# Sample attention ahead of the prompt's blocks, and the last prompt block between layer 1's expert slots

## The chip, the cores and the metric

The kernel runs on one core of one Trainium2 chip. The time is that of one execution on the device, in microseconds (us). Three runs of the kernel before took 3454.8, 3460.62 and 3466.63 us; the median is 3460.62 us. The engines are TensorE (PE, with its weight loads as PEld), VectorE (DVE), ScalarE (ACT), GpSimd (POOL) and SyncE (SP), which only issues DMAs. Each runs its own instructions in the order of the program and waits on semaphores for the others.

## The reference

One inference step of a two-layer decoder for 512 prompt tokens and 8 sample tokens (rows of 1024 floats). What matters here:

```python
x = s5_layer(x)                     # layer 0: state space mixer
x = x + ga2 * peer(h, layer 0)      # experts
ckv, kr = shared_kv(x)              # latent keys and values, 256 + 32 wide
# layer 1: latent attention, 16 heads
s = (q_lat . ckv + q_pe . kr) * SM_SCALE   # causal, in blocks of 128 queries, for the prompt
o = softmax(s) . ckv                       # the samples: over 2048 paged cache rows and their own
x = x + ga1 * (o . w_ukv) @ w_o
x = x + ga2 * peer(h, layer 1)
def peer(h):                        # 8 heads, top 16 of 128 x 128 keys each: 128 experts a token
    s = (h @ w_q) . sub_keys; idx, g = top_k(top_k(s, 16) pairs, 16), softmax
    u, v = u_emb[idx], v_emb[idx]   # rows of 1024 floats each
    return sum_k g * gelu(h . u) * v
```

## The kernel before

**The expert stage.** The 512 prompt tokens are four tiles of 128 tokens, the samples are a fifth, smaller tile; `t` counts them over both layers, 0 to 4 in layer 0 and 5 to 9 in layer 1. A prompt tile has 128 slots, one for each chosen expert: in a slot, POOL's indirect DMA (L1133) fetches a row of `peer_uv` for each of the 128 tokens (1 MB: 128 partitions, 2048 floats), DVE makes the dot product (L2143), ACT the gelu, its gate and a diagonal (L1411, L1421, L1424), and PE adds the value rows with 16 matmuls (L2747). The rows lie in a ring of six buffers; slot m+6 is fetched when PE has freed the buffer of slot m. What is computed for the next tile (norm, turn, 16 `query` groups L2681, `score` L2707, and `top` on DVE L2059 ff, in six parts for a head) is spread by `peer_plan` (L457) over the slots of the tile that runs: a list of steps that each engine walks, doing those that are its own. `PLAN[0]` is layer 0's, `PLAN[1]` layer 1's.

**The stretch between the layers.** With the last tiles of layer 0 most of the projections of attention are already computed. Between the two lists stand hand written sequences, one for each engine: `attention_sync` (L1036, SP), `attention_pool` (L1156), `attention_act` (L1612), `attention_dve` (L2337) and `attention_pe` (L2912). Their order is: the samples' latent queries (L2918); 8 key products (L2928); 4 value products (L2942); then a pipelined loop over 64 head steps, 16 heads in each of prompt blocks 0 to 3 (block i sees i+1 tiles of keys): scores L2958 and mask L2962 on PE, maximum L2363 on DVE, exponential L1638 on ACT, reciprocal L2368 on DVE, scaling L1154 on POOL (`scaled_probabilities`), transposes L2972 on PE, copies L2375 on DVE, and the product with the values L3067 on PE, a pair of heads at a time (`pair_outputs`). After each block follows the output projection `project` (L3107, L3116) and `attention_out` on DVE. Then come the samples, one after the other over 2048 cache rows each (`cache_turn` L3085, `cache_scores` L3098 and L3102, L3001, L3014); their rows are fetched by POOL (L1174, L1177) into three buffers. `merge` joins the partial sums (L3019 to L3050), `sample_project` (L3130) projects them. The norm, the first query group, the first score and the first head's `top` of tile 5 are computed during the samples and the merge (the list `EARLY`). Layer 1's gathers start when the first head's experts are known.

SP fetches prompt queries, weights and rows in the order of its own list; a wait there holds back all that follows.

## Time and profile before

| | us |
|---|---|
| median of three runs (3454.8 to 3466.63) | 3460.62 |
| the profiled execution | 3468.7 |
| its span, first to last instruction | 3466.6 |
| PE busy in it | 2561.7 |
| DVE busy in it | 2331.3 |
| ACT busy in it | 1252.6 |
| POOL busy in it | 1239.8 |
| mean granted TensorE clock, share of full | 0.804 |

The span holds both expert stages, which the indirect DMAs fill, and what lies before, between and after them. Stretches are given in us from the start of the span. A line of a timeline has start, duration, engine, line, operation and its operands, the count, and in brackets the idle time before it with what ended it.

### The profile page before, as it was taken

The numbers are of one execution on the slowest core, as the hardware profiler recorded it, in microseconds if no ns is written. First come the engines' busy times: TensorE is split into PE (matmuls) and PEld (weight loads), VectorE is DVE, ScalarE is ACT, GpSimd is POOL, SyncE is SP. The second block draws the span as 40 slices with busy tenths as digits, with TensorE's granted clock in tenths as the row PEclk, the third lists the DMA queues.
The fourth block names the chain that finished last, engine by engine and source line by source line (L and its number), as shares of the span: only waits on it lengthen the run. The fifth ranks groups of instructions, "written<-read, shape, count | busy, mean of one in ns | idle before, by whom it ended". The sixth has DMA issues, their size and how long they took to land.

```text
span 3466.6 us, 62653 instructions
## 1 busy us (share of the span) xinstructions
PE 2561.7 (74%) x25173; PEld 936.6 (27%) x25173; DVE 2331.3 (67%) x5471; ACT 1252.6 (36%) x3861; POOL 1239.8 (36%) x1133
## 2 busy tenths in 40 slices
PE   4878997767668766668889986686686677666666
PEld 3756322323003100112235563240040023001000
DVE  8753885897775776465644455978767767775655
ACT  3442333333333333344432232433433343334333
POOL 0010343444444444334413512344444444443432
PEclk8979998878778766779998998797686678667677
DMA  9966999999999999999950157999999999999997
GB/s 321 354 228 269 394 419 415 409 400 407 426 425 409 413 426 423 408 414 410 389 176 29 74 213 314 403 408 421 426 397 426 426 423 411 427 424 403 422 427 318
DMA packets 182783, 1276.32 MB, mean 368 GB/s; under 512 B 22200, under 2 KB 27808, under 8 KB 35544
## 3 DMA queue, kind: packets, MB, share of 16 engines
q0 software_dynamic: 151696, 1109.99, 77.6%
q1 hardware_dynamic: 30224, 161.80, 12.5%
q8 instruction: 195, 3.19, 0.3%
q14 instruction: 92, 0.75, 0.1%
q10 hardware_dynamic: 576, 0.59, 0.0%
HBM read 1260.89 MB, written 11.40 MB: 367 GB/s over the span
## 4 chain that ended last, share of the span: by engine, by line
DMA 37%; PE 36%; DVE 18%; ACT 6%; issue 3%; POOL 1%; SPq 0%; DVEq 0%; ACTq 0%; PEldq 0%; POOLq 0%
DMA arena<-peer_uv,arena 35%; PE psum L2747 12%; DVE arena L2143 8%; PE psum L2681 7%; PE psum L2640 3%; PE psum L3116 2%; DMA arena<-b_mod 2%; PE psum L2897 1%; PE psum L2828 1%; ACT arena L1424 1%; ACT arena L1421 1%; DVE arena L2154 1%; PE psum L2508 1%; DVE arena L2059 1%; DVE arena L1714 1%
## 5 line engine op out<-in xcount | busy, mean ns | idle before, releaser
L2747 PE MATMUL psum<-arena 32*32 32x512 f32 x16384 | 1491.5, 801 | 743.7 <-ACT arena L1424 733.2
L1133 POOL DMA_INDIRECT arena<-peer_uv,arena x1040 | 1134.9, 1091 | 1782.6 <-PE psum L2747 1527.7
L2143 DVE SCALAR_TENSOR_TENSOR arena<-arena 128x1024 f32<-128x1024 f32 x1040 | 1272.4, 1225 | 730.4 <-DMA arena<-peer_uv,arena 716.1
L1411 ACT ACTIVATE arena<-arena 128x1 f32<-128x1 f32 x1040 | 210.3, 202 | 1528.8 <-DVE arena L2143 1524.1
L2747 PEld LDWEIGHTS psum<-arena 32*32 32x32 f32 x16384 | 214.9, 118 | 1877.6 <-ACT arena L1424 1771.9
L1424 ACT ACTIVATE arena<-arena 128x32 f32<-128x32 f32 x1024 | 329.1, 321 | 33.4
L1421 ACT ACTIVATE arena<-arena 128x1 f32<-128x1 f32 x1040 | 306.0, 294 | 33.8
L2681 PEld LDWEIGHTS psum<-arena 128*128 128x128 f32 x2048 | 244.9, 197 | 78.7 <-issue 75.8
L2681 PE MATMUL psum<-arena 128*128 128x128 f32 x2048 | 263.9, 285 | 2.7 <-ACT arena L1363 2.2
L2640 PE MATMUL psum<-arena 128*128 128x512 f32 x256 | 126.7, 628 | 3.2 <-ACT arena L1321 2.4
L2508 PE MATMUL psum<-arena 128*9 128x128 f32 x2048 | 82.3, 325 | 59.4 <-DMA arena<-b_mod 59.3
L1154 POOL TENSOR_SCALAR arena<-arena 128x128 f32<-128x128 f32 (+3 forms) x64 | 68.8, 1082 | 93.9 <-DVE arena L2368 93.2
L1714 DVE TENSOR_TENSOR arena<-arena 128x512 f32<-128x512 f32 (+9 forms) x177 | 89.3, 505 | 8.7 <-ACT arena L1201 2.8
L2143 DVE DVE_READ_ACCUMULATOR arena<-arena 128x1 f32 x1040 | 84.8, 82 | 0.0
L2508 PEld LDWEIGHTS psum<-arena 128*9 128x9 f32 x2048 | 62.3, 106 | 75.2 <-issue 43.0
L1638 ACT ACTIVATE arena<-psum,arena 128x128 f32<-128x128 f32 (+3 forms) x64 | 33.7, 527 | 105.9 <-DVE arena L2363 105.7
L2059 DVE MAX8 arena<-arena 128x8 f32<-128x128 f32 (+1 forms) x204 | 61.8, 331 | 13.1 <-ACT arena L1456 10.8
L2640 PEld LDWEIGHTS psum<-arena 128*128 128x128 f32 x256 | 45.8, 194 | 83.8 <-issue 79.4
L2059 DVE FIND_INDEX8 arena<-arena 128x8 uint32<-128x128 f32 (+1 forms) x204 | 65.5, 329 | 0.0
L2061 DVE FIND_INDEX8 arena<-arena 128x8 uint32<-128x128 f32 (+1 forms) x204 | 65.5, 329 | 0.0
L2060 DVE MATCH_REPLACE8 arena<-arena 128x128 f32<-128x128 f32 (+1 forms) x204 | 64.2, 320 | 0.0
L1223 ACT ACTIVATE arena<-psum 9x128 f32<-9x128 f32 x128 | 34.4, 269 | 76.7 <-PE psum L2513 74.2
(350 smaller groups left out, 2298.2 us busy)
## 6 DMA issues: line engine op xcount, KB each, us to landing
arena<-w_mod SPq DMA_DIRECT2D x64, 1024.0 KB
arena<-peer_wq SPq DMA_DIRECT2D x12, 2048.0 KB, 11.6
arena<-peer_uv,arena POOLq DMA_INDIRECT x1040
arena<-w_glu SPq DMA_DIRECT2D x5, 2048.0 KB
arena<-mod_rows SPq DMA_DIRECT2D x4, 1024.0 KB
arena<-w_o SPq DMA_DIRECT2D x1, 4096.0 KB
arena<-mod_rows SPq DMA_DIRECT2D x7, 512.0 KB
arena<-x_after_layer SPq DMA_DIRECT2D x7, 512.0 KB
```

Of the source, the lines that this page charges most:

```text
L1133: pool.indirect_dma_start(ring[r], None, a[f"peer_uv{t // 5}"], bass.IndirectOffsetOnAxis(ap=ix, axis=0)).then_inc(landed[r], 16)
L1411: act.activation(col, col, ACT.Gelu_apprx_tanh).then_inc(s_gl, 1)
L1421: act.activation(wcol, col, ACT.Copy, scale=gate_).then_inc(s_gl, 1)
L1424: act.activation(diag[:, n_ % RING, :], eye32, ACT.Copy, scale=wcol).then_inc(s_dg, 1)
L1714: link(dve.tensor_tensor(out, x, y, op))
L2059: steps = (lambda x, v, i: dve.max(v[:, 0:8], x), lambda x, v, i: dve.max_index(i[:, 0:8], v[:, 0:8], x), lambda x, v, i: dve.match_replac ...
L2143: dve.scalar_tensor_tensor(out=u, in0=u, scalar=1.0, in1=h, op0=ALU.mult, op1=ALU.mult, accum_out=at(DOTS + (t % 2) * 2 * P + m, 1)).then_ ...
L2508: ins = pe.matmul(mod_bank(b, q, one), silu[:, k, :], w[k // 4][:, k % 4, MQ4 * q:MQ4 * (q + 1)], start=(k == 0), stop=False, skip_group_c ...
L2640: ins = pe.matmul(psum[:, unit_bank(u), :], ztk[:, k, P * j:P * (j + 1)], w[:, k, :], start=(k == 0), stop=(k == KD - 1))
L2681: ins = pe.matmul(psum[:, 4 + m % 2, P * q:P * q + R], (wq[:, m, k] if t else wide(WQ0[m])[:, k])[:, P * q:P * (q + 1)], htr[:, k, 0:R], s ...
L2747: ins = pe.matmul(acc_of(t, i, c), diag[rows, r, :], ring[r][rows, D + 512 * c:D + 512 * (c + 1)], start=(m == 0), stop=last, skip_group_c ...
L3116: ins = pe.matmul(psum[:, 5 + n_, :], ot[:, k, :], wo[:, k, 512 * n_:512 * (n_ + 1)], start=(k == 0), stop=(k == KD - 1))
```

## The change

The stretch between the layers is put in another order, and a part of it is moved into layer 1's expert stage.

The samples come first, right after their latent queries; the key products are spread over the merge, the value products lie around the samples' projection. Then comes a new list, `exposed_blocks`, of 48 head steps for prompt blocks 0 to 2, as `PLAN[1]`. From its step 21 on it also holds the whole front of tile 5: norm, turn, 16 query groups (with two buffers of their own for the weights, in the ring), four scores, and `top` of heads 0 and 1. Layer 1's first six gathers are issued after the 48th scaling on POOL. Block 3 (16 heads, projection in four pieces) becomes steps in the first 46 slots of tile 5 (`blocks_in_stream`); the other six heads of `top` of tile 5 follow at 2.4 slots a part, those of tile 6 are split between tile 5 and tile 6. The head steps 16 to 47 use two score banks for three, and one transpose bank for two. SP reads block 3's queries back from memory as it does those of the other blocks; layer 1's query weights are fetched twice: in pieces for tile 5 between the layers (8 MB), and again for tiles 6 to 9 during the slots of tile 5 (8 MB). Of these 16 MB the kernel before fetches 8.

```diff
-            first = [[] for _ in range(64)]
-            prep(t0, first, 0)
-            ahead = 21 if layer else 26
-            for steps in first[:ahead]:
-                plan += steps
-            plan += [("top", t0, 0, part) for part in range(6)]
...
+                if t == 5:
+                    blocks_in_stream(extra)
+                    for m in range(36):
+                        extra[1 + int(2.4 * m)].append(("top", t, 2 + m // 6, m % 6))
+                    for m, h0 in ((29, 2), (60, 4), (90, 6)):
+                        extra[m].append(("shift", t, h0, h0 + 2))
+                        extra[m + 1].append(("exps", t, h0, h0 + 2))
+                        extra[m + 2].append(("gates", t, h0, h0 + 2))
...
-                    at_ = 73 if t == 0 else 40 if b == 0 else 10
+                    at_ = 73 if t == 0 else 76 if b == 0 else 10
                     prep(t + 1, extra, at_)
                     at_ += 22 if b < 3 else 30
-                    gap = 1.25 if t == 0 else 1.3 if b == 0 else 1.5 if b == 3 else 1.75
-                    heads = 4 if t == 0 else heads_of(t + 1)
+                    gap = 1.25 if t == 0 else 1.1 if b == 0 else 1.5 if b == 3 else 1.75
+                    heads = 4 if b == 0 else heads_of(t + 1)
                     for m in range(6 * heads):
...
-        EARLY = ([(what, 5) for what in ("squares", "means", "roots", "norm", "shifted", "turned")]
-                 + [("turn", 5, 0), ("turn", 5, 1), ("queried", 5, 0), ("score", 5, 0), ("scored", 5, 0)]
-                 + [("query", 5, 0, q) for q in range(4)] + [("top", 5, 0, part) for part in range(6)])
-        PLAN = [peer_plan(0), [step for step in peer_plan(1) if step not in EARLY]]
...
+        INS = 3
+        EXPOSED = INS * NH
...
+        def blocks_in_stream(extra):
+
+            for i in range(INS, NTILE):
+                base = 1 if i == INS else 41
+                for p in range(NH // 2):
+                    n, s = NH * i + 2 * p, base + 4 * p
+                    extra[s].append(("pscore", n))
+                    extra[s + 1].append(("pscore", n + 1))
+                    extra[s + 3] += [("pmax", n), ("pmax", n + 1)]
+                    extra[s + 4] += [("pscale", n), ("pscale", n + 1)]
+                    extra[s + 5].append(("pturn", n))
+                    extra[s + 7] += [("pturned", n), ("pturn", n + 1)]
+                    extra[s + 9] += [("pturned", n + 1), ("pvalue", n // 2)]
+                    if p % 4 == 3:
+                        extra[s + 11].append(("pheads", n // 8))
+                for piece in range(4):
+                    extra[base + 40 + piece].append(("project", i, piece))
+                extra[base + 45].append(("pout", i))
...
+        def exposed_blocks():
+
+            t, plan, queries = 5, [], [("query", 5, m, q) for m in range(4) for q in range(4)]
+            side = [[] for _ in range(EXPOSED + 8)]
+            side[21] += [("squares", t), ("means", t)]
+            side[22] += [("roots", t), ("norm", t)]
+            side[23] += [("shifted", t), ("turn", t, 0), ("turn", t, 1), ("turned", t)]
+            for k, step in enumerate(queries):
+                side[24 + k // 2].append(step)
+                if step[3] == 3:
+                    m = step[2]
+                    side[24 + k // 2].append(("queried", t, m))
+                    side[25 + k // 2] += [("score", t, m)]
+                    side[26 + k // 2] += [("scored", t, m)]
+            for k in range(12):
+                side[29 + k // 2].append(("top", t, k // 6, k % 6))
+            side[35] += [("shift", t, 0, 2), ("exps", t, 0, 2), ("gates", t, 0, 2)]
+            for it in range(EXPOSED + 8):
+                if it < EXPOSED:
+                    plan += [("pscore", it), ("pmax", it)]
+                if it >= 5 and it % 2 and it - 5 < EXPOSED:
+                    p = (it - 5) // 2
+                    plan.append(("pvalue", p))
+                    if p % 4 == 3:
+                        plan.append(("pheads", p // 4))
+                if 1 <= it <= EXPOSED:
+                    plan.append(("pscale", it - 1))
+                if 3 <= it < EXPOSED + 3:
+                    plan += [("pturn", it - 3), ("pturned", it - 3)]
+                if it % NH == 4 and it >= NH:
+                    i = it // NH - 1
+                    plan += [("project", i, piece) for piece in range(4)] + [("pout", i)]
+                plan += side[it]
+            return plan
...
+        def pscore_bank(n):
+
+            if n < NH:
+                return (0, 1, 7)[n % 3]
+            return (n + 1) % 2 if n < EXPOSED else 4 + n % 2
+
+        def pturn_bank(n):
+
+            if n < NH:
+                return 2 + 4 * (n % 2)
+            return 2 if n < EXPOSED else 6
+
+        def pvalue_bank(p):
+            return 3 if 2 * p < EXPOSED else 7
+
+        def project_bank(i):
+            return 6 if i >= INS else 4
+
+        BLOCKS = 1
...
+        PLAN = [peer_plan(0), exposed_blocks(), peer_plan(1)]
...
-                for dst, src, rows in ((WK, "w_k", P), (WV, "w_v", P), (WKT, "w_kt", NOPE)):
+                for dst, src, rows in ((WV, "w_v", P), (WKT, "w_kt", NOPE)):
                     n_ = a[src].shape[1]
                     sp.dma_start(at(dst, n_, 0, rows), a[src]).then_inc(s_lw, 16)
+                queries_spill(3)
...
+                for g in range(4):
+                    sp.dma_start(at(X4, 256, 32 * g, 32 * g + NB), x2s_dram[:, 256 * g:256 * (g + 1)]
+                                 ).then_inc(s_mw, 16)
+                    sp.dma_start(at(GAS4, 256, 32 * g, 32 * g + NB),
+                                 mod_dram[1:NC9, 8 * D + 256 * g:8 * D + 256 * (g + 1)]).then_inc(s_mw, 16)
                 sp.dma_start(at(WO, KD * D), a["w_o"]).then_inc(s_mw, 16)
...
+                sp.dma_start(at(WK, 2 * NH * NOPE), a["w_k"]).then_inc(s_mw, 16)
+                sp.dma_start(at(GAP, D), mod_dram[0:1, 8 * D:9 * D].partition_broadcast(P)).then_inc(s_mw, 16)
+
                 sp.wait_ge(s_cpv, NB)
+                block_queries(0)
+                first_query_weights(0)
+                first_query_weights(1)
+                sp.wait_ge(s_mg, 7)
+                block_queries(1)
+                sp.dma_start(at(SSB, D), a["g_norm"][3:4, :].partition_broadcast(P)).then_inc(s_pmod, 16)
+                sp.wait_ge(s_ktp, NH // 2)
+                sp.dma_start(at(PMOD, 2 * D), mod_dram[0:1, 9 * D:11 * D].partition_broadcast(P)
+                             ).then_inc(s_pmod, 16)
+                sp.wait_ge(s_vp, NTILE)
+                block_in(0)
+                block_in(1)
+                sp.wait_ge(s_mh, 2)
                 peer_keys(1)
-                sp.wait_ge(s_yy, 5)
-                peer_weights(1, 2)
-                peer_weights(1, 3)
-                attention_store(4)
-                for i in range(2):
-                    sp.wait_ge(s_rst[i], row_no(STORES, "residual", 4 - i))
-                    sp.wait_ge(s_kvs[i], 32 * (3 - i))
-
-            def attention_store(j):
-                sp.wait_ge(s_x3, j + 1)
-                if j < 4:
-                    sp.dma_start(x3_dram[P * j:P * (j + 1)], at(MX + (j % 2) * D, D)).then_inc(s_rst[j % 2], 16)
-                    return
+                sp.wait_ge(s_x3, 1)
                 for g in range(4):
                     sp.dma_start(x3s_dram[:, 256 * g:256 * (g + 1)], at(X4, 256, 32 * g, 32 * g + NB)
                                  ).then_inc(s_rst[0], 16)
+                block_out(0)
+                sp.wait_ge(s_S, NH)
+                block_queries(2)
+                sp.wait_ge(s_pq, 21)
+                first_query_weights(2)
+                sp.wait_ge(s_pq, 22)
+                first_query_weights(3)
+                sp.wait_ge(s_ph, 6)
+                block_stored(0)
+                block_in(3)
...
+            def blocks_beside_experts(load):
+
+                block_out(2)
+                block_stored(2)
+                load(6)
+                sp.wait_ge(s_S, 4 * NH)
+                peer_weights(1, 0)
+                peer_weights(1, 1)
+                sp.wait_ge(s_pv, NTILE * NH // 2)
+                final_loads()
+                sp.dma_start(at(HSP, D), a["g_norm"][3:4, :].partition_broadcast(P)).then_inc(s_pmod, 16)
+                sp.wait_ge(s_yy, NTILE + 1)
+                peer_weights(1, 2)
+                peer_weights(1, 3)
+                block_out(3)
+                sp.wait_ge(s_kvs[0], 96)
+                sp.wait_ge(s_kvs[1], 64)
+                sp.wait_ge(s_rst[0], row_no(STORES, "residual", 4))
+                sp.dma_start(at(PMOD + 2 * D, D), mod_dram[0:1, 11 * D:12 * D].partition_broadcast(P)
+                             ).then_inc(s_pmod, 16)
+                sp.dma_start(at(PMOD + 3 * D, 3 * D, 0, NB), mod_dram[1:NC9, 9 * D:12 * D]).then_inc(s_pmod, 16)
+                block_stored(3)
+                load(5)
 
             peer_tiles(0, x1_dram, x1s_dram, x2_dram, x2s_dram)
             attention_sync()
-            peer_loads(1)
             peer_tiles(1, x3_dram, x3s_dram, a["out_y_p"], a["out_y_s"])
...
                 for b in range(NB):
                     if b == 1:
-                        scaled_probabilities()
-                        pool.wait_ge(s_pv, NTILE * NH // 2)
-                    if b == 3:
-                        pool.wait_ge(s_rz, 1)
+                        pool.memset(at(QRZ, NB * P), 0.0).then_inc(s_rz, 1)
+                        pool.wait_ge(s_qsp, 64)
...
+            def second_gather(k):
+
+                t, m = (5 + k // P, k % P) if k < NTILE * P else (9, k - NTILE * P)
+                if t == 9:
+                    if m == 0:
+                        pool.wait_ge(s_sld, 32)
+                    gather(t, m, at(IXS, SGRP).bitcast(I32)[:, m:m + 1])
+                    return
+                if m % TOPK == 0:
+                    pool.wait_ge(s_idx, 8 * t + m // TOPK + 1)
+                if k < RING:
+                    r = slot_no(t, m) % RING
+                    if r >= 4:
+                        pool.wait_ge(s_S, NH * (3 if r == 4 else 2))
+                    else:
+                        pool.wait_ge(s_pq, 23 + r // 2)
+                gather(t, m, at(IDXP + (t % 2) * P, P).bitcast(I32)[:, m:m + 1])
+
+            def second_gathers():
+                total, k = NTILE * P + SGRP, RING
+                for ahead in range(RING):
+                    second_gather(ahead)
+                for what, *which in PLAN[2]:
+                    if what == "pscale":
+                        scaled_probabilities(*which)
+                    elif what == "slot" and k < total:
+                        second_gather(k)
+                        k += 1
 
             peer_gathers(0)
             attention_pool()
-            peer_gathers(1)
+            blocks_pool()
+            second_gathers()
```

## Rows read from the trace of the kernel before

**Rows 1.** The page, 40 slices of the span: what the DMA engines moved.
```profile
GB/s 321 354 228 269 394 419 415 409 400 407 426 425 409 413 426 423 408 414 410 389 176 29 74 213 314 403 408 421 426 397 426 426 423 411 427 424 403 422 427 318
```

**Rows 2.** Busy time by stretch; the last columns are the clock, DMA share, GB/s.
```profile
1900.00:2000.00 100.00, 91.61 (x523) 52.25 (x522) 45.79 (x98) 23.66 (x61) 44.42 (x33) 0.99 0.18 69
2400.00:2500.00 100.00, 66.88 (x648) 9.03 (x640) 80.92 (x178) 43.03 (x133) 43.46 (x40) 0.67 1.01 422
```

**Rows 3.** POOL's timeline around the stretch between the layers.
```profile
1732.32 1.86 POOL L1133 DMA_INDIRECT arena<-peer_uv,arena  x1 [2.31 <-PE psum L2752]
...
1928.92 2.81 POOL L1154 TENSOR_SCALAR arena<-arena 128x384 f32<-128x384 f32 x2 [1.12 <-DVE arena L2368]
...
2102.06 0.94 POOL L1133 DMA_INDIRECT arena<-peer_uv,arena  x1 [46.95 <-DVE arena L2109]
...
2121.87 1.14 POOL L1133 DMA_INDIRECT arena<-peer_uv,arena  x1 [12.67 <-PE psum L2747]
```

**Rows 4.** PE's timeline of the same stretch.
```profile
1804.02 1.92 PE L2918 MATMUL psum<-arena 64*8 64x256 f32 x32 [1.79 <-ACT arena L1604]
1805.87 14.00 PE L2928 MATMUL psum<-arena 128*128 128x512 f32 x32
...
1834.32 0.38 PE L2958 MATMUL psum<-arena 96*128 96x128 f32 x2
...
1858.92 13.90 PE L3116 MATMUL psum<-arena 128*128 128x512 f32 x32
...
2003.37 1.92 PE L3098 MATMUL psum<-arena 128*32 128x512 f32 x16
...
2079.65 0.27 PE L3019 MATMUL psum<-arena 128*8 128x128 f32 x1
...
2081.14 3.84 PE L2681 MATMUL psum<-arena 128*128 128x128 f32 x32 [1.11 <-ACT arena L1363]
...
2091.07 1.16 PE L2707 MATMUL psum<-arena 128*128 128x128 f32 x8
...
2103.30 6.23 PE L3130 MATMUL psum<-arena 128*8 128x256 f32 x64 [0.31 <-ACT arena L1670]
```

**Rows 5.** DVE's timeline: attention_out's last pass, the first head's top, a dot.
```profile
1995.15 1.23 DVE L2488 TENSOR_TENSOR arena<-arena 128x1024 f32<-128x1024 f32 x1
...
2093.24 0.48 DVE L2059 MAX8 arena<-arena 128x8 f32<-128x128 f32 x2
...
2101.62 0.17 DVE L2109 SCALAR_TENSOR_TENSOR arena<-arena 128x16 int32<-128x16 f32 x1
...
2112.89 1.22 DVE L2143 SCALAR_TENSOR_TENSOR arena<-arena 128x1024 f32<-128x1024 f32 x1
```

**Rows 6.** The cache gathers of L1174, issue to landing, all eight.
```profile
DMA to landing us min/median/max: 7.9/8.2/11.6
```

**Rows 7.** DMA issues from 1700 to 2200 us: layer 1's query weights.
```profile
arena<-peer_wq SPq DMA_DIRECT2D x4, 2048.0 KB, 7.1
```

**Rows 8.** Busy time by stretch, columns as rows 2: block 3, the start of layer 1.
```profile
1949.40:1977.90 28.50, 25.84 (x218) 16.62 (x216) 19.47 (x39) 9.04 (x23) 18.62 (x12) 1.00 0.05 20
...
2100.00:2125.00 25.00, 19.39 (x202) 11.62 (x202) 14.18 (x48) 5.77 (x17) 7.97 (x9) 0.85 0.86 348
```

**Rows 9.** ACT's timeline beside slots: an exponential between two gelus.
```profile
2243.70 1.28 ACT L1403 ACT_TABLE_LOAD   x1
2245.00 0.26 ACT L1403 ACTIVATE arena<-arena 128x64 f32<-128x64 f32 x1
2245.27 1.28 ACT L1411 ACT_TABLE_LOAD   x1
```

**Rows 10.** PE beside a tile's query groups: one slot, half its queries, the next slot.
```profile
2529.93 1.09 PE L2747 MATMUL psum<-arena 32*32 32x512 f32 x16
...
2530.95 2.05 PE L2681 MATMUL psum<-arena 128*128 128x128 f32 x16
...
2532.93 1.09 PE L2747 MATMUL psum<-arena 32*32 32x512 f32 x16
```

683 lines of the change are left out of this document (359 added, 324 removed).

## The prediction, made before the changed kernel ran

> **What bounds the kernel now.** I read the page's slices first: the DMA engines move some 400 to 427 GB/s through most of the span, with one hole in the middle [rows 1]. The stretches say how deep: in steady slots the DMA share is 1.01 at 422 GB/s, with PE busy 67% and DVE 81%, while between the layers it is 0.18 and PE is busy 92% [rows 2]. So the expert stages run at the gathers' pace: 40 gathers in 100 us, 2.5 us each [rows 2]. POOL's timeline gives the hole's edges: layer 0's last gather is issued at 1732.3, layer 1's first at 2102.1 [rows 3], and from there to the end of the span are 1364.5 us. Only two things can change the time: when that first gather leaves (I call it G), and what the rest costs after it, in bytes or in slots that fall behind.
>
> The sum is made against the profiled span, 3466.6 us; the execution took 3468.7, and the median of the runs, 3460.6, lies 6.0 below the span. Layer 0 keeps its list, and up to 1804 only loads and a store of SP change, which nothing on that path waits for; I cost it at nothing, at worst 2 us.
>
> **The new G, stage by stage.** The starting point is the latent queries at 1804.0 [rows 4].
>
> *Samples.* Before, from the first sample's scores at 2003.4 to the merge at 2079.7 are 76.3 us [rows 4]; about 1 of them is tile 5's turn, which goes. New is that the cache rows must land first. The gather is issued at about 1803. Landing takes 7.9 to 11.6 us [rows 6], the long one beside w_o; here w_o is issued some 4 us behind it, so I take 9: PE waits until 1812 (bounds 1811 to 1815). Nothing hides this; what was hidden there (keys and values) is now later. For the first sample's turns, copies and latent transposes ahead of its scores I take what a whole further sample takes, 76.3 / 8 or about 10 us: 1822. Then 75.3: the merge begins at 1897 to 1898. The second and third cache rows, w_o and w_k are some 11 MB in the queue at 1808, 27 us at 422 GB/s, against a need at about 1835: 0 to 5 us, I take 1. 1898.
>
> *Merge with keys.* Keys cost 14.0 us on PE [rows 4]. The merge itself: from 2079.7 to the samples' projection at 2103.3 are 23.7 us, less two times two query groups (7.7), the score (1.2) and the wait for `top` (2093.2 to 2101.8) leaves about 6 [rows 4, 5]. The keys take the query groups' place as filler. 19.5 together, to 1917.5.
>
> *Values and the samples' projection.* Values take as much as keys, 14. The projection's 6.23 us [rows 4] ran behind G and now stand ahead of it. With transposes 20.5, to 1938; DVE's last copy and the masks add 2: head steps run from 1940.
>
> *48 head steps.* Before, they ran from 1834.3 to the 48th scaling, the first of the two in the row at 1928.9, which ends at about 1930 [rows 3, 4]: 96 us, with two projections of 13.90 in them. The third projection and block 3 fall behind G: that is the gain. Fewer banks put a copy between two transposes, which lies beside the next scores; PE was idle a tenth of the loop [rows 8], so I allow nothing to 0.15 us for each of 32 steps, bounds 0 and 5, and take 1.
>
> *Tile 5's front in them.* At steps 21 to 23: norm, shift and the scale's preparation are four DVE passes of about 1.2 us (as the 1.23 of [rows 5]), behind a square root on ACT with its table, 1.3 us each way [rows 9]; 5.5 us. From 24 to 31 PE has 16 query groups, 3.84 us for four [rows 4], 15.4 in all, and 4 scores of 1.16. DVE does two heads of `top` in steps 29 to 34; one head takes 8.5 us, 2093.2 to 2101.8 [rows 5], so 17. Head steps tie the engines together within one or two steps, so the fuller engine sets each: PE in steps 24 to 28 (5 steps of 1.9 for queries and 0.6 for scores, 12.5, less 1 for its idle share), DVE in 29 to 34 (17 less 1.3, which hide the other queries): 27. The third and fourth weight pieces are fetched when a buffer is free; 7.1 us to land [rows 7] against two steps of together 7 us (1.4 a step of the loop's own and 2.5 of the front's): 1. Gates, by the step's own size, 1.5. Together 35, bounds 22 (PE's work alone) and 44.
>
> G = 1940 + 96 + 1 + 35 = 2072, 30 earlier than before.
>
> **After G.** Before, this took 1364.5 us. Four things are added.
>
> *More bytes.* Before, query weights 2 and 3 (4 MB), mods, gains and rows, 8.6 MB, are loaded behind G. Now it is all four weights again (8 MB) and the rest, 13.1. The difference, 4.5 MB (4.7 million bytes), costs 11 us at 422 GB/s; no cover, as DMA is the bound. Bounds 8 and 13.
>
> *A hole behind the first six.* Six gathers are 15 us of DMA. Before, PE freed the first buffer 19.8 us after G (2121.9) [rows 3], and weights filled the gap: the first 25 us, 2 of them ahead of G, average 348 GB/s [rows 8]. Now, behind the 48th scaling come the last transposes and values (two head steps and a copy, 3.4 us), the third projection (13.9 [rows 4]) and attention_out (2 x 1.23 [rows 5]): DVE's first dot stands at G+20 (before G+10.8 [rows 5]), behind it ACT, PE and the issue take some 5 us, and data flows again at about G+26.5 against a drained queue at G+17. A row of 0.5 MB comes in between: 9 us lost, bounds 5 and 12.
>
> *Block 3 in 45 slots.* Its loop took 25.8 us of PE in 28.5 [rows 8] for three quarters of the heads, some 37 us for all with projection apart. For every 4 slots (10 us) PE has 4 x 1.09 [rows 10] and 4.6 for two heads, 9.0; DVE has 4 dots of 1.22 [rows 5], 1.67 parts of `top` (8.5 / 6 each) and 2.7 for two heads (19.5 of DVE less 2.5 of attention_out for 12 or 13 heads [rows 8]), 10.0; POOL 4 gathers of 0.94 [rows 3] and two scalings of 1.5 (18.6 for 12 [rows 8]), 6.8. DVE is just full, but behind the 31st slot 8 MB of weights slow the gathers and it catches up. The projection puts 3.5 us on PE in each of 4 slots, while the ring holds 15 us. I take 4 us, bounds 0 and 24.
>
> ACT now alternates between gelu and exp: the row shows 1.28 us for a table and the next activation 1.30 after its start, both ways [rows 9]. Eight pairs of heads make 16 loads, 21 us, beside 112 us of slots in which ACT is under half busy [rows 2]; they cost nothing, or 2 us. The Trainium skill, in "ScalarE: Activation LUTs", section "Table sets: the hidden batching unit", has a rule against this part ("Batch activation calls by set, not by function"), and its section "What ACT_TABLE_LOAD costs" puts 2.66 us to a switch with its drain. The row shows 1.30, so the trace does not agree with the larger figure; by the Trainium skill's figure the 16 loads would be an estimated 43 us of ACT, still beside other work.
>
> *Less work later.* Twelve parts of `top` leave the slots. They were under the gathers: nothing.
>
> After G: 1364.5 + 11 + 9 + 4 = 1388.5. End: 2072 + 1388.5 = 3460.5, 6 under the old span; against the median 3454.6, rounded 3454.
>
> **The rivals.**
>
> *The stretch between is shorter.* PE idles about a tenth of the head steps, and part of the queries and of `top` may fall into those gaps (25 us for the front of tile 5 in place of 35), the samples run without tile 5's steps and wait less (4 less), the hole is 5. For it: PE's busy share there was 25.8 of 28.5 [rows 8], so there is room. Against it: in steps 29 to 34 DVE alone has its 17 us, and the list is in order. 3454 - 10 - 4 - 4 = 3436.
>
> *The mixed slots become the bound (slower).* Place: PE and DVE in slots 1 to 45 of tile 5. Where a tile's queries stand beside slots, PE's cycle is 3.0 us from one slot to the next (2529.9 to 2532.9) although its parts are 1.09 and 2.05 [rows 10]; the same order of work, scores, transposes, values, waits among them, might hold block 3's slots at 3.1. It decides once four slots take over 10 us on PE or on DVE; DVE has nothing to spare, and a wait for the exponential (1.3 + 2 x 0.9) stands in its list. Price: 0.6 x 45 = 27 in place of 4: 3454 + 23 = 3477. Against it: PE's average is under the pace, and six buffers even it out.
>
> *The change does not bring the samples forward as it says*: the first cache rows queue behind w_o and the spill, and the next ones behind these. Price 10 us, if w_o's 4 MB and the two others go first; 3464. For it: the 11.6 us landing [rows 6]. The Trainium skill, in "DMA: Bandwidth & Descriptors", section "SWDGE vs HWDGE vs iDMA", says that an engine goes round robin between its queues, so a gather would not stand behind w_o, but share with it; no row here shows the order within an engine.
>
> **How the numbers follow.** Forecast (3444 to 3466) 0.47, the shorter stretch 0.28, mixed slots 0.19, late cache rows 0.06. A difference of under about 0.3%, 10 us, can't be told from none in this kernel: that is 3450 to 3471. Of the forecast 0.10 lies under 3450. Faster: 0.28 + 0.10 = 0.38. Slower: 0.17 of the mixed slots, 0.02 of the late rows: 0.19. The same: 0.43. The range takes in the short stretch with the bounds of the front's cost (3430) and the mixed slots to their price (3477): 3430 to 3477. The likeliest case's own range is 3444 to 3466.
>
> **What the profile of the changed kernel would show.** The first cache turn on PE at about 1812, the first merge transpose near 1898, the first L2958 scores near 1940, and POOL's first peer gather at 2072 (2056 for the shorter stretch, over 2080 for late cache rows). A DMA share well under 1 for about 9 us from G+17. In the first 110 us of slots DMA at 400 GB/s or more; if PE or DVE is the bound, the share falls to 0.8 to 0.9 and DVE waits for PE or ACT, not for the gathers. From there to the end, the same pace as before. The prediction is wrong if G lies outside 2060 to 2085, or if what follows G is outside 1378 to 1400 us.

## The result, and the profile after

The changed kernel took 3488.4 us (median of four runs, 3484.1 to 3493.9) against 3457.7 for the kernel before (median of four): the medians lie 30.7 us apart, and the ratio with its 95% interval is put at 1.0075 (1.005 to 1.010), which is 26 us. It is slower by 26 to 31 us, where 3454 had been forecast, and the time lies above the range of 3430 to 3477. Its profiled execution took 3490.1 us with a span of 3487.9 and a mean granted clock of 0.803.

The page's slices answer [rows 1]. The hole between the layers has moved forward, and at its end stands a slice of 321 that lies wholly behind the first gather (2092 to 2180 us); four slices on, one of 382 is new.

```profile
GB/s 319 346 233 273 397 419 416 414 402 410 426 424 408 421 426 425 409 419 398 351 186 211 80 101 321 410 418 404 382 405 424 426 417 410 426 424 380 423 427 320
```

PE's timeline answers [rows 4]. To read in it: the latent queries at 1798.0, the wait for the first cache rows (11.36 us on a DMA), the merge at 1899.7, the keys, values from 1919.3, the first block's scores at 1937 to 1939, and then in the head steps the query groups of tile 5 (L2836) and their score (L2865).

```profile
1798.01 1.92 PE L3088 MATMUL psum<-arena 64*8 64x256 f32 x32 [1.78 <-ACT arena L1754]
1811.29 3.65 PE L3279 MATMUL psum<-arena 128*128 128x128 f32 x16 [11.36 <-DMA arena<-cache_kr,arena]
1827.70 4.53 PE L3279 MATMUL psum<-arena 128*128 128x128 f32 x20 [4.84 <-DMA arena<-cache_kr,arena]
1899.71 0.27 PE L3134 MATMUL psum<-arena 128*8 128x128 f32 x1
1900.38 3.67 PE L3196 MATMUL psum<-arena 128*128 128x512 f32 x8 [0.29 <-ACT arena L1791]
1919.26 7.13 PE L3206 MATMUL psum<-arena 128*128 128x512 f32 x16
1938.83 0.23 PE L3231 MATMUL psum<-arena 128*128 128x128 bf16 x1 [1.36 <-DVE arena L2521]
...
2003.52 3.74 PE L2836 MATMUL psum<-arena 128*128 128x128 f32 x32
2007.94 1.16 PE L2865 MATMUL psum<-arena 128*128 128x128 f32 x8
2008.94 3.74 PE L2836 MATMUL psum<-arena 128*128 128x128 f32 x32
```

POOL's timeline answers [rows 3]: the first gather of layer 1 at 2080.3 (before 2102.1), the first refill of the ring 27.3 us behind it (before 19.8), and a pair of block 3's scalings (L1269) between the gathers, on the same engine.

```profile
2080.28 1.01 POOL L1249 DMA_INDIRECT arena<-peer_uv,arena  x1 [0.16 <-issue]
...
2107.57 1.30 POOL L1249 DMA_INDIRECT arena<-peer_uv,arena  x1 [20.07 <-PE psum L2909]
2110.40 0.94 POOL L1249 DMA_INDIRECT arena<-peer_uv,arena  x1 [1.53 <-PE psum L2909]
...
2120.45 3.11 POOL L1269 TENSOR_SCALAR arena<-arena 128x512 f32<-128x512 f32 x2
2123.72 0.99 POOL L1249 DMA_INDIRECT arena<-peer_uv,arena  x1 [0.17 <-issue]
```

Two lengths carry the comparison, since layer 0's end moves from one profiled execution to the next: the latent queries came at 1798.0 and 1810.1 in two profiles of the changed kernel. The **front** is the time from the latent queries to the first gather of layer 1 (G): 298.0 us before [rows 3, 4], 282.3 after. The **tail** is the time from G to the end of the span: 1364.5 before, 1407.6 after. The front gained 15.7, the tail lost 43.1, and the two make +27.4, about what the whole times show. (From 1804.0 the forecast had 268 for the front and 1388.5 for the tail.)

Where the tail lost it is read from the gathers, one a slot, numbered from G in POOL's timeline. Us after G:

| gather | before | after |
|---|---|---|
| 16 | 52.9 | 56.8 |
| 32 | 102.0 | 103.5 |
| 48 | 144.8 | 155.8 |
| 64 | 185.5 | 212.3 |
| 96 | 266.2 | 292.8 |
| 128 (tile 6's first) | 345.0 | 375.0 |
| 144 | 387.0 | 426.0 |
| end of the span | 1364.5 | 1407.6 |

30.0 us go by gather 128, another 9.1 in tile 6's first 16 slots, and 4.1 in all the rest (0.6 in a second profile of the changed kernel, so this part is no loss). The stretches between gathers of the table (columns as in [rows 2]), first of after, gathers 0 to 16, 16 to 48, its two halves 16 to 32 and 32 to 48, 128 to 144, and the bottom of the dip; then of before, gathers 128 to 144:

```profile
2080.28:2137.06 56.78, 43.52 (x301) 16.03 (x297) 30.75 (x72) 22.43 (x55) 25.30 (x20) 0.88 0.78 297
2137.06:2236.08 99.02, 73.90 (x711) 27.27 (x709) 72.61 (x186) 51.42 (x133) 56.44 (x44) 0.88 0.97 382
2137.06:2183.78 46.72, 36.58 (x381) 14.44 (x379) 39.23 (x95) 29.04 (x73) 32.17 (x25) 0.93 0.94 355
2183.78:2236.08 52.30, 37.32 (x332) 12.83 (x331) 33.38 (x92) 22.38 (x62) 24.26 (x20) 0.84 1.00 406
2455.24:2506.30 51.06, 29.09 (x264) 3.98 (x272) 45.63 (x117) 21.30 (x60) 19.35 (x16) 0.57 0.96 378
2100.00:2110.00 10.00, 5.18 (x38) 1.11 (x36) 9.30 (x25) 2.46 (x9) 1.30 (x1) 0.83 0.37 116
```

```profile
2447.03:2489.03 42.00, 27.84 (x272) 4.04 (x272) 31.86 (x51) 22.52 (x62) 17.90 (x16) 0.65 1.01 425
```

The first two rows are the stretch in which block 3 sits. 32 slots took 99.0 us, **3.09 us a slot**, where [rows 2] have 2.5. The two halves differ: 2.92 us a slot at a share of 0.94, then 3.27 at a share of 1.00 and 406 GB/s, when two planes of query weights (4 MB, issued at 2194) come beside the gathers. So the engines hold back the transfers in the first 32 slots, and in the next 16 the transfers are full. In tile 6's first slots VectorE is busy 45.6 of 51.1 us, before 31.9 of 42.0: the 24 parts of `top` that now stand there at 1.2 slots each.

The DMA answer over 128 gathers gives the bytes, after first and then before:

```profile
DMA packets 19878, 145.55 MB, mean 388 GB/s; under 512 B 2201, under 2 KB 2201, under 8 KB 3097
```

```profile
DMA packets 19355, 141.28 MB, mean 410 GB/s; under 512 B 2170, under 2 KB 2202, under 8 KB 2714
```

4.27 MB more cost 10.4 us at 410 GB/s (an estimate); the other 19.6 of the 30.0 are the lower rate.

What VectorE waits for longest between 2137 and 2183 us, in total, times and longest; after, after between 2183 and 2236 us, and then before:

```profile
DVE arena L2555 <- PE psum L3247: 6.0, 2, 3.8
```

```profile
DVE arena L2278 <- DMA arena<-peer_uv,arena: 16.1, 7, 5.1
```

```profile
DVE arena L2143 <- DMA arena<-peer_uv,arena: 11.5, 8, 2.6
```

Before, VectorE waited for gathers, so the transfers were the bound. After, it waits for none in the first of its stretches; it waits for TensorE's transposes of block 3 (L3247). In the second it waits for gathers again, 16.1 us. One turn of the loop is seen whole in the timeline of all engines (start, duration, engine, line):

```profile
2130.66 4.46 POOL L1269 TENSOR_SCALAR arena<-arena 128x512 f32<-128x512 f32 x2
...
2133.16 1.28 ACT L1809 ACT_TABLE_LOAD   x1
2133.63 0.66 PE L3247 MATMUL psum<-arena 128*128 128x128 f32 x4 [1.54 <-POOL arena L1269]
...
2134.32 0.69 DVE L2555 COPY arena<-psum 128x512 f32<-128x512 f32 x1 [2.09 <-PE psum L3247]
2134.93 1.28 DVE L2539 TENSOR_REDUCE arena<-psum 128x1 f32<-128x512 f32 x2
...
2135.64 0.69 ACT L1809 ACTIVATE arena<-psum,arena 128x512 f32<-128x512 f32 x1 [1.20 <-DVE arena L2539]
...
2137.11 1.28 ACT L1557 ACT_TABLE_LOAD   x1
...
2138.40 0.20 ACT L1557 ACTIVATE arena<-arena 128x1 f32<-128x1 f32 x1
...
2139.34 1.09 PE L2909 MATMUL psum<-arena 32*32 32x512 f32 x16 [1.68 <-ACT arena L1570]
...
2140.77 0.94 POOL L1249 DMA_INDIRECT arena<-peer_uv,arena  x1 [1.37 <-PE psum L2909]
```

Each bracket names the engine above it: TensorE's transpose waits for POOL's scaling, VectorE's copy for the transpose, the exponential for VectorE's maxima, the slot's matmul for ScalarE behind the table load that follows the exponential, and the gather for that matmul. No engine is full (TensorE is busy 75% and VectorE 73% of these 32 slots), and each works through its list in order, so a wait for one block step also holds back the expert slot that stands behind it.

### The profile page after: what moved, and what is told of

Read it like the earlier page. It is cut to its first block and busy times, and to the rows that moved or that the text cites. A ratio compares the mean times of both kernels' runs of the same rounds, so it can differ in the third digit from the quotient of the medians.

```text
span 3487.9 us, 62696 instructions
## 1 busy us (share of the span) xinstructions
PE 2562.2 (73%) x25173; PEld 938.6 (27%) x25173; DVE 2330.3 (67%) x5474; ACT 1274.6 (37%) x3880; POOL 1251.7 (36%) x1133
## 5 line engine op out<-in xcount | busy, mean ns | idle before, releaser
L1570 ACT ACTIVATE arena<-arena 128x32 f32<-128x32 f32 x1024 | 329.1, 321 | 33.4
L2836 PE MATMUL psum<-arena 128*128 128x128 f32 x2048 | 259.5, 282 | 1.1 <-ACT arena L1509 1.1
L2836 PEld LDWEIGHTS psum<-arena 128*128 128x128 f32 x2048 | 241.9, 195 | 68.4 <-issue 66.7
L1269 POOL TENSOR_SCALAR arena<-arena 128x128 f32<-128x128 f32 (+3 forms) x64 | 73.2, 1148 | 134.5 <-DVE arena L2546 133.3
L1809 ACT ACTIVATE arena<-psum,arena 128x128 f32<-128x128 f32 (+3 forms) x64 | 33.5, 526 | 102.5 <-DVE arena L2539 102.3
## 6 DMA issues: line engine op xcount, KB each, us to landing
arena<-peer_uv,arena POOLq DMA_INDIRECT x1040, 10.2
```

The lines of the kernel that those rows point to most:

```text
L1269: pool.tensor_scalar(pp, pp, at(SUMS + n_ % 16, 1), None, ALU.mult).then_inc(s_sc, 1)
L1570: act.activation(diag[:, n_ % RING, :], eye32, ACT.Copy, scale=wcol).then_inc(s_dg, 1)
L2836: ins = pe.matmul(psum[:, 4 + m % 2, P * q:P * q + R], (wq1[m][:, k] if t == 5 else wq[:, m, k] if t else wide(WQ0[m])[:, k])[:, P * q:P * ...
```

## The experiments

All start from the changed kernel. Lengths are from one profiled execution each; the changed kernel was run twice (*control*), and its two profiles give 282.3 and 281.3 for the front, 375.0 and 374.3 for gather 128, 1407.6 and 1403.4 for the tail. The tail holds to about 4 us, and the ratio to the kernel before has intervals of about 0.25% either way. Gather 128 is the sharpest measure, but less sharp than these two profiles make it. Seven kernels that change nothing ahead of G (*spread6*, *turnlate*, *notable*, *dve2*, *pe2*, *copy_act*, *relief*) show a front of 278.3 to 279.0. The same head steps ran there at a mean granted clock of 0.91 and in the changed kernel at 0.89, which took 3.3 us more from the masks to G. In these seven the ring's first refill also comes 25.7 us behind G and not 27.3. So differences of under 2 us at gather 128 are read as none.

| kernel | front | gather 16 | 32 | 48 | 128 | 128 to 144 | tail | ratio to before |
|---|---|---|---|---|---|---|---|---|
| before | 298.0 | 52.9 | 102.0 | 144.8 | 345.0 | 42.0 | 1364.5 | 1 |
| after | 282.3 | 56.8 | 103.5 | 155.8 | 375.0 | 51.1 | 1407.6 | 1.0075 [1.0050, 1.0100] |
| control | 281.3 | 56.8 | 104.4 | 155.9 | 374.3 | 51.1 | 1403.4 | 1.0082 [1.0052, 1.0112] |
| ins4 | 328.4 | 61.6 | 100.8 | 140.1 | 342.4 | 51.4 | 1370.4 | 1.0122 [1.0092, 1.0151] |
| spread6 | 278.3 | 54.1 | 98.0 | 145.6 | 378.8 | 52.4 | 1406.0 | 1.0083 [1.0057, 1.0109] |
| proj2 | 281.8 | 40.4 | 89.7 | 144.6 | 371.6 | 51.0 | 1401.0 | 1.0080 [1.0053, 1.0108] |
| balanced | 282.8 | 55.8 | 104.7 | 158.2 | 376.7 | 45.4 | 1397.5 | 1.0060 [1.0037, 1.0083] |
| late3 | 282.7 | 50.0 | 89.2 | 138.5 | 377.9 | 51.5 | 1404.3 | 1.0103 [1.0083, 1.0123] |
| turnlate | 278.6 | 53.1 | 100.7 | 152.3 | 372.1 | 51.1 | 1406.1 | 1.0098 [1.0077, 1.0118] |
| scale_act | 282.0 | 55.2 | 100.6 | 154.2 | 373.0 | 52.0 | 1400.6 | 1.0085 [1.0058, 1.0111] |
| notable | 278.4 | 54.2 | 98.1 | 151.1 | 370.5 | 51.5 | 1397.8 | 1.0067 [1.0046, 1.0087] |
| dve2 | 278.3 | 57.2 | 107.7 | 159.5 | 378.9 | 51.1 | 1408.1 | 1.0102 [1.0073, 1.0132] |
| pe2 | 279.0 | 54.6 | 104.1 | 157.0 | 377.4 | 51.4 | 1402.8 | 1.0080 [1.0046, 1.0114] |
| copy_act | 278.4 | 55.9 | 107.0 | 158.8 | 379.4 | 52.2 | 1409.4 | 1.0081 [1.0057, 1.0105] |
| tiny | 282.8 | 49.4 | 92.4 | 144.2 | 364.2 | 51.4 | 1392.8 | 1.0042 [1.0022, 1.0062] |
| relief | 278.3 | 50.2 | 91.5 | 143.9 | 364.7 | 51.0 | 1391.3 | 1.0035 [1.0019, 1.0051] |
| wqhole | 282.8 | 63.2 | 111.0 | 160.6 | 379.7 | 51.0 | 1407.5 | 1.0101 [1.0074, 1.0128] |
| front2q | 307.1 | 54.9 | 102.8 | 154.7 | 376.4 | 51.1 | 1406.5 | 1.0156 [1.0117, 1.0195] |
| combo3 | 273.6 | 42.2 | 93.7 | 141.8 | 368.3 | 45.1 | 1389.2 | 1.0000 [0.9978, 1.0022] |
| combo4 | 273.7 | 42.1 | 89.0 | 137.0 | 361.4 | 45.1 | 1381.7 | 0.9997 [0.9981, 1.0012] |

> The changed kernel again, for the spread of the two stretches between profiled executions: from the latent query to the first gather of layer 1 282.3, from there to the end 1407.6. Every theory expects both again within 4 us, and the time within 3482 to 3496.

The front and gather 128 held, the tail at the edge of the 4 us; the median, 3495.3, stood against 3466.5 for the kernel before beside it.

**Is it block 3 in the slots?** *ins4* puts block 3 back between the samples and the first gather and keeps all else.

```
-        INS = 3
+        INS = 4
```

> The changed kernel with INS = 4: block 3 goes back between the layers as head steps 48 to 63 of the exposed list, nothing of it lies in tile 5's slots. G is the issue of layer 1's first gather (2080.3 in the changed kernel), R what follows it to the end of the span (1407.6; before 1364.5). Theory A (of R's 43 us more, about 13 are block 3 in the slots and 10 a hole of the DMA behind the first six gathers): G rises by 16 heads (37) and the third projection (14) to about 2131, R falls to about 1385, as weights can fill the hole; time 3518. Theory B (the repeated 8 MB and DMA traffic alone make R long, the mixed slots cost nothing): R stays at 1400 or more, time 3532 or more.

Its windows over gathers 0 to 16 and 16 to 32:

```profile
2132.32:2193.95 61.63, 37.41 (x255) 11.05 (x258) 24.63 (x59) 11.70 (x38) 15.85 (x16) 0.72 1.00 414
2193.95:2233.17 39.22, 23.71 (x256) 3.06 (x240) 28.90 (x71) 13.07 (x48) 16.99 (x16) 0.75 1.01 426
```

The transfers never let up: no dip and no slow slots, although the same query weights are loaded again. The ring's first refill is nearly as late as in the changed kernel (26.5 us behind G), but here block 3's scores are done early, so SP issues the first two planes of weights 4 us ahead of G and the other two 20 us behind it:

```profile
2128.12 0.81 SPq L981 DMA_DIRECT2D arena<-peer_wq  x2
```

These bytes fill the gap. The tail is 1370.4, only 6 over before's, although tile 6's first slots take 9 more. So block 3 in the slots, with the later weights that come of it, costs the tail 33 to 37 us (gather 128: 375.0 against 342.4), while the front is 46.1 longer without it (328.4 against 282.3). Theory A had the direction and not the size (1385 and 3518 said, 1370.4 and 3504.7 measured). The move of block 3 brings 9 to 14 us by itself, of the 46 that it takes from the front. And the rest of the change, which *ins4* has too, costs 36 us by the profiles (30.4 in the front, where all of tile 5's front now stands ahead of G, and 5.9 in the tail): that is why the whole is slower although this move pays. The row also gives the price of a slot at full rate: 39.22 / 16 = 2.45 us.

**Is it the dip at the start?** Three kernels. *late3* starts block 3's steps at slot 29, *spread6* puts six slots instead of four between pairs of heads, *proj2* puts block 2's projection into slots 1 to 4 and starts block 3 at slot 8.

```
 late3    -                base = 1 if i == INS else 41
          +                base = 29 if i == INS else 41
 spread6  -                    n, s = NH * i + 2 * p, base + 4 * p
          +                    n, s = NH * i + 2 * p, base + 6 * p
          -                    extra[base + 40 + piece].append(("project", i, piece))
          +                    extra[base + 54 + piece].append(("project", i, piece))
 proj2    +                for piece in range(4):
          +                    extra[1 + piece].append(("project", i - 1, piece))
          +                extra[7].append(("pout", i - 1))
          +                base = 8
```

> Block 3's steps start at tile 5's slot 29 instead of slot 1, so that the ring is filled beside plain slots with only the tops of heads 2 to 7 in them. Theory H (the hole at the start of the stream, where six slots come at once, is most of the loss): gather 32 comes at 108 to 111 after the first (before: 102.0) whatever the blocks do, and from there on the pace is that of the transfers; total unchanged or 0 to 5 less. Theory P or T (the mixed slots themselves are slower than the transfers): gather 28 at 98 or earlier, then 48 slots that again take 12 to 18 us more than the transfers need, gather 128 at 366 to 375 and the whole 1398 to 1408.

> The changed kernel with block 3's pairs of heads six slots apart in place of four (projection in slots 55 to 58). Theory A (the slots lose because DVE, PE and ACT together are full for 31 slots): each slot carries a third less, R falls by 6 to 10, time 3480. Theory B (each pair costs its waits and table loads however it is spaced): no change, 3486 to 3491.

> The changed kernel with block 2's projection out of the exposed list: its four pieces stand in tile 5's slots 1 to 4, its attention_out at slot 7, and block 3 starts at slot 8. Theory A (DMA stands idle from G+17 to G+27 because DVE's first dot waits for that projection): DVE's first dot at G+5, second round of gathers from about G+8, no hole; R falls by 9, time 3479. Theory B (the engines then are the bound in the first slots, so that the hole only moves): R falls by under 3, time 3485 to 3490.

*late3*, gathers 0 to 16, 16 to 32 and 48 to about 80:

```profile
2094.91:2144.91 50.00, 34.28 (x246) 11.07 (x250) 24.23 (x59) 11.70 (x38) 16.13 (x17) 0.83 0.78 310
2144.91:2184.09 39.18, 23.72 (x256) 3.13 (x240) 28.98 (x71) 13.09 (x48) 16.33 (x16) 0.75 1.01 426
2233.40:2338.00 104.60, 78.94 (x700) 27.83 (x708) 74.37 (x183) 47.94 (x128) 56.07 (x42) 0.85 0.97 384
```

This splits the loss. With plain slots behind it, and no weights to fill it, the dip costs 50.0 - 39.2 = 10.8 us, and the pace is full directly after. Then the slots with block 3 in them run at 3.27 us each (104.6 / 32, the weights among them), and by gather 128 nothing is won. *spread6* is quicker to gather 48 and has given it back by gather 128, as its theory B said. *proj2* took 16 us off the first 16 slots and had 3 left at gather 128; its tail, 1401.0, lies between its two theories. Theory H, that the dip is the whole loss (gather 32 at 108 or later in *late3*), falls: gather 32 came at 89.2. The dip is some 11 us of it, and moving work about within the slots does not remove the rest.

**Which engine?** Six kernels take work off one engine of the mixed slots or add to it. *turnlate* sets each transpose one slot later; *scale_act* moves the scaling from POOL to ScalarE; *notable* computes Exp in place of Gelu in 46 slots, which takes the table loads away (some 18 of 1.28 us in the changed kernel, not the 30 of its expectation); *copy_act* moves the 16 copies from VectorE to ScalarE; *dve2* computes each maximum twice; *pe2* each value product twice.

```
 turnlate   -                    extra[s + 5].append(("pturn", n))
            +                    extra[s + 6].append(("pturn", n))
            (and the copies, values and heads one slot later with it)
 scale_act  +                    elif what == "pscale" and which[0] >= EXPOSED:
            +                        act.activation(pp, pp, ACT.Copy, scale=at(SUMS + n_ % 16, 1))
 notable    -                act.activation(col, col, ACT.Gelu_apprx_tanh)
            +                act.activation(col, col, ACT.Exp if t == 5 and m < 46 else ACT.Gelu_apprx_tanh)
 copy_act   +                    elif what == "pturned" and which[0] >= EXPOSED:
            +                        turned_by_scalar(*which)
 dve2       +                if n_ >= EXPOSED:
            +                    dve.tensor_reduce(at(SUMS + 16 + n_ % 16, 1), psum[:, bank, 0:w], AX.X, ALU.max, negate=True)
 pe2        -                for k in range(i + 1):
            +                for k in [*range(i + 1)] * (2 if 2 * p >= EXPOSED else 1):
```

> Block 3's transposes, copies and value products stand one slot later in tile 5's slots (six slots after the scores instead of five), nothing else. In the changed kernel TensorE waited at the transpose (L3247) for GpSimd's scaling (L1269) and VectorE waited up to 3.8 us for the transpose. Theory P (in-order coupling: TensorE holds back the expert slots' matmuls behind a transpose whose scaling GpSimd does only after its gathers): the 1407.6 us from the first gather of layer 1 to the end fall by 6 to 12, gather 128 comes at 363 to 369 us after the first instead of 375. Theory T (the activation table loads, two a pair, pace the slots) and theory H (the unfilled ring at the start is the loss): within 3 us of 1407.6.

> The scaling of block 3's probabilities is issued on ScalarE (an activation Copy with the reciprocal as scale) instead of on GpSimd, so that GpSimd has only the gathers in tile 5. It takes 1.93 us each off GpSimd and puts about 0.7 each on ScalarE, which is 65% busy there. Theory P: 1407.6 falls by 6 to 12, and the gathers no longer stand 3 to 4.5 us behind a pair of scalings. Theory T: ScalarE is the engine that paces, and 0.7 x 16 more on it makes the stretch 0 to 8 us longer. Theory H: no change.

> In the first 46 expert slots of tile 5 the gate's Gelu is replaced by Exp (this changes what those 46 slots compute), so that ScalarE need not load an activation table before and after each pair of exponentials: some 30 loads of 1.28 us go, 38 us of ScalarE's time. Theory T: 1407.6 falls by 10 or more and gather 64 comes at 200 or earlier instead of 212. Theory P: the loads lie in ScalarE's idle time, change under 4. Theory H: no change.

> Each of block 3's 16 score maxima is computed twice, the first into spare columns: 16 x 0.68 = 10.9 us more on VectorE inside tile 5's slots 1 to 46 and nothing else. Theory D (VectorE paces these slots): the stretch from the first gather of layer 1 to the end, 1407.6 in the changed kernel, grows by 8 to 11. Theory E (TensorE paces them): by 0 to 3. Theory L (no engine alone; each waits in turn for the others' results, a loop through all four engines' program orders): by 3 to 8.

> Each of block 3's 8 pairs of value products (16 steps' matmuls of 128x64 against 128x128, 1.09 us a pair) is computed twice: 8 x 1.09 = 8.7 us more on TensorE in tile 5's slots. Theory D: the stretch grows by 0 to 3. Theory E: by 7 to 9. Theory L: by 2 to 7.

> The 16 copies of block 3's transposed probabilities (0.69 us each, L2555) go from VectorE to ScalarE: 11 us off VectorE, about 0.68 x 16 = 11 us on ScalarE. Theory D: the stretch falls by 8 to 11. Theory E: no change. Theory L: from 6 less to 4 more, since ScalarE stands in the same loop (dot, Gelu, diagonal, TensorE).

By gather 128, against 374.3 and 375.0: turnlate -3, scale_act -2, notable -4, dve2 +4 for 10.9 us of work, pe2 +3 for 8.7 us, copy_act +5. Between gathers 16 and 48 the two doublings took 102.3 and 102.4 us in place of 99.0. All but *scale_act* are among the seven with the earlier refill, which may stand for up to 1.6 us: the gains of *turnlate* and *notable* may be that much smaller, the losses of the others that much larger. *scale_act*'s 2 is at the edge of the spread. Most expectations were given for the tail, and there the answers are no clearer than its spread: dve2 1408.1, pe2 1402.8, copy_act 1409.4, against 1403.4 and 1407.6, by which theory E would stand for *dve2* and D for *pe2*. Nor does any of the six whole times leave the interval of the control. At gather 128 no engine's work comes back in full, and the doublings do not come back as nothing. Theories D, E, P and T each asked for more from one engine; theory L (every engine in one loop) is what is left, at the lower end of what it had expected, about a third of each us. Each of these sizes comes from one profile.

**Do the reliefs add, and is it the work or the order?** *relief* is notable, scale_act and turnlate in one; *tiny* keeps every step, wait and table load of block 3 and cuts its work to 32 columns.

```
 tiny  +                if n_ >= EXPOSED:
       +                    pe.matmul(psum[:, bank, 0:32], qblk[i][0:QKD, h, :], kt_[0:QKD, h, 0:32], start=True,
       +                              stop=False, skip_group_check=True)
       -                w = P * (n_ // NH + 1)
       +                w = P * (n_ // NH + 1) if n_ < EXPOSED else 32
```

> Three reliefs that each moved the stretch by 2 to 10 us alone, together: no table loads in tile 5's first 46 slots (Gelu replaced by Exp there, which changes what those slots compute), block 3's scaling on ScalarE instead of GpSimd, its transposes one slot later. Theory W (the sum of the work on coupled engines, each with a sensitivity of about a third): they add, gather 128 at 364 to 367, the stretch 1390 to 1396. If one common cause stood behind all three: no better than the best alone, 370 and 1398.

> Every step of block 3 keeps its place, its waits and its signals, and its two activation table loads a pair, but works on 32 columns instead of 512 (scores, maxima, exponentials, scaling, copies), one transpose instead of four and two value matmuls instead of eight: the attention output of block 3 is left out by it. Theory W (work): the mixed slots are slow because the four engines' work for block 3 adds up with that of the slots; then most of the 33 us that the first 128 gathers take longer (375.0 against 342.4 with block 3 exposed) goes, gather 128 at 345 to 352, the stretch 1378 to 1385. Theory S (order and waits: each slot waits in turn for steps that stand before it on another engine, and table loads): gather 128 stays at 360 or later, the stretch at 1393 or more.

*relief* over gathers 0 to 16, 16 to 32 and 32 to 48, and what VectorE waited for longest between 2120 and 2167 us:

```profile
2075.77:2125.99 50.22, 40.01 (x280) 14.41 (x276) 28.88 (x70) 15.69 (x50) 16.44 (x17) 0.90 0.81 306
2125.99:2167.25 41.26, 35.09 (x380) 13.21 (x376) 37.92 (x94) 23.24 (x71) 17.10 (x16) 0.96 1.01 425
2167.25:2219.72 52.47, 34.65 (x348) 11.70 (x345) 35.45 (x95) 19.36 (x65) 17.37 (x16) 0.87 1.01 420
```

```profile
DVE arena L2284 <- DMA arena<-peer_uv,arena: 1.2, 2, 0.7
```

Singly the three gave 3, 2 and 4; together 10. Within the spread they add. The slots of gathers 16 to 32 run at 41.26 / 16 = 2.58 us, at a share of 1.01: the transfers are full there again, and VectorE hardly waits (1.2 us for gathers, 1.0 and 0.8 for TensorE). *tiny* gives as much, 10.5, by the work alone. Here the whole times agree: 3477.2 and 3476.8 against 3495.3 for the control beside them. Neither gets near 345: behind gather 32 the row has a share of 1.01 at 420 GB/s, so now the weights' bytes are the limit, and the dip is left. For *relief* theory W's numbers hold. For *tiny* neither theory's do cleanly: gather 128 at 364.2 is in S's range and the tail at 1392.8 just under it, far from W's 345 to 352, while the quicker slots show that the work was the loop's part of the loss.

**Do bytes moved to the start of the stream come free?** *wqhole* cuts two weight planes (4 MB, issued at 2194 in the changed kernel) to 64 columns and instead stores 4 MB of keys, issued behind block 2's store and the next row's load.

```
+                sp.dma_start(copy_dram, at(KT, NH * SEQ)).then_inc(s_pw, 16)
                 sp.wait_ge(s_S, 4 * NH)
-                peer_weights(1, 0)
-                peer_weights(1, 1)
+                for m in range(2):
+                    sp.dma_start(at(WQ + m * KD * HQ // 4, 64), a["peer_wq"][1][:, m * KD * HQ // 4:m * KD * HQ // 4 + 64])
```

> Moves 4 MB from behind the mixed slots to the dip at the start of the stream: the two query-weight planes of 2 MB each that the changed kernel can load only when block 3's scores are done (2194, when the transfers are at full rate) are cut to 64 columns each (so layer 1's later queries use stale weights), and in their place 4 MB of the key buffer are written out to memory at 2106, where the changed kernel moves 116 to 330 GB/s. Theory B (the lost time is the transfers': bytes that in the kernel before lay ahead of the first gather or in the dip now come at full rate, and the dip stays empty): 4 MB less at 0.42 MB/us is 10 us less behind gather 32 and little more ahead of it: gather 128 at 366 to 368 against 374.3 and 375.0, the stretch 1394 to 1398 against 1403.4 and 1407.6. Theory L (the engines' in-order loop is the bound throughout): no change, gather 128 at 372 or later.

The issue of the store, the stretch ahead of it, and the windows over gathers 0 to 16, 16 to 32 and 32 to 48:

```profile
2118.09 0.43 SPq L1202 DMA_DIRECT2D keys_copy<-arena  x1
2109.00:2118.10 9.10, 4.27 (x17) 1.46 (x23) 5.43 (x15) 0.82 (x3) 0.00 (x0) 0.95 0.27 111
2092.27:2155.47 63.20, 48.09 (x301) 16.57 (x298) 30.94 (x72) 22.32 (x55) 23.35 (x20) 0.81 0.85 341
2155.47:2203.26 47.79, 36.02 (x381) 13.53 (x379) 39.73 (x95) 28.91 (x73) 32.91 (x24) 0.93 0.90 338
2203.26:2252.86 49.60, 37.13 (x332) 12.47 (x332) 34.29 (x93) 22.41 (x62) 26.86 (x20) 0.86 0.97 371
```

Theory B failed at both ends. Gather 16 came 6.4 us later. But the store missed the bottom of the dip: it was issued 25.8 us behind G, after the 9 us at 111 GB/s and 1.5 us ahead of the first refill (G+27.3), so it ran beside the refill, and VectorE waited 7.4 us for gathers in those 16 slots, where it had waited for none. Whether the empty 10 us would have taken bytes for free this run does not show; *ins4*, whose weights fill them, says that they do. And where 4 MB less are moved the slots hardly quickened: 49.6 us against 51.5 and 52.3 for gathers 32 to 48, 3.10 us each, at 371 GB/s; over gathers 32 to 64 104.6 against 107.1 and 108.8, where 10 had been expected. So in the mixed slots the loop alone would hold about 3.1 us, and most of those 4 MB had been hidden there. Theory L's bound (gather 128 at 372 or later) holds, though its "no change" does not: 379.7.

**The step that mis-sized the front.** *front2q* computes tile 5's 16 query groups twice.

```
-                for k in range(KD):
+                for k in [*range(KD)] * (2 if t == 5 else 1):
```

> Each of the 16 query groups of tile 5 that stand beside blocks 1 and 2 is computed twice (8 more matmuls of 128x128 a group, the same result). The step that the prediction mis-sized: it took a group at 3.84/4 = 0.96 us, by which 16 more cost 15.4. If a row of 32 records is two groups, a group is 1.92 us and the first gather comes 30.7 later, so that 282.3 from the latent query to the first gather becomes 311 to 314. If VectorE and not TensorE were the bound there, 0 to 10. The stretch behind the first gather doesn't change.

```profile
2009.20 7.31 PE L2836 MATMUL psum<-arena 128*128 128x128 f32 x64
2017.20 1.16 PE L2865 MATMUL psum<-arena 128*128 128x128 f32 x8
```

The row of a head step has 64 records for two groups of 8 matmuls done twice: each matmul leaves two records, so a row of x32 is two groups, 1.87 to 1.92 us a group. The first gather came 24.8 to 25.8 us later (307.1 against 282.3 and 281.3), where 30.7 had been expected. That is 1.6 us a group, four fifths of TensorE's time for it; 0.96 a group would have given 15.4.

**A version that beats both?** *balanced* moves tops: tile 5's at 2.0 slots a part, six of tile 6's heads instead of four in tile 5. It also lets a shift write over a scratch buffer that a head's choice still needs, which changes some of tile 5's chosen experts; the same steps in *combo3* and *combo4* stand where that does not happen. *combo3* joins the balanced tops, proj2, scale_act and tile 5's first two tops one head step earlier, at three parts a step; *combo4* adds turnlate.

```
-            for k in range(12):
-                side[29 + k // 2].append(("top", t, k // 6, k % 6))
-            side[35] += [("shift", t, 0, 2), ("exps", t, 0, 2), ("gates", t, 0, 2)]
+                side[28 + k // 3].append(("top", t, k // 6, k % 6))
+            side[32] += [("shift", t, 0, 2), ("exps", t, 0, 2), ("gates", t, 0, 2)]
-                        extra[1 + int(2.4 * m)].append(("top", t, 2 + m // 6, m % 6))
+                        extra[1 + int(2.0 * m)].append(("top", t, 2 + m // 6, m % 6))
-                    heads = 4 if b == 0 else heads_of(t + 1)
+                    heads = 4 if t == 0 else 6 if b == 0 else heads_of(t + 1)
```

> The changed kernel with the top steps spread otherwise: tile 5's own 36 parts at 2.0 slots, tile 6's front from slot 53 with six heads at 1.35 slots in tile 5, and only two heads at 2.3 slots in tile 6 (was four at 1.2). Theory A (the 10 us lost between gathers 128 and 144, where DVE is 97% busy, are DVE's): that loss goes, at most 2 us come elsewhere, time 3480. Theory B (the loss there is tile 6's start itself, sums and norms of two tiles): no change, 3486 to 3491.

> Four corrections at once: tile 5's two exposed tops begin one head step earlier, three parts a step (first gather 8 us earlier); block 2's projection in tile 5's first slots (measured alone: the stretch after the first gather 6.6 less); the tops of heads 2 to 7 of tile 5 at 2.0 slots a part and two more heads of tile 6 taken out of tile 6's first slots (about 10 less); block 3's scaling on ScalarE (7 less). If they add up: first gather at about 2072 with the sample steps starting at 1798, the stretch about 1384, the time 3457, level with the kernel before. If the mixed slots take back what is put into them (theory L): stretch 1390 to 1398, time 3464 to 3475.

> The four corrections of the combination (tops of tile 5 one head step earlier, block 2's projection in the first slots, tops spread and taken out of tile 6's first slots, scaling on ScalarE) and block 3's transposes one slot later. If the late transpose adds to them as it did alone (gather 128 3 us earlier): stretch 1384 to 1387, time 3460 to 3463, ratio to the kernel before 0.998 to 0.999. If not: as the combination, 1.000.

Tile 6's first slots fell from 51.1 to 45.4 and 45.1 us with half the parts of `top` in them, so VectorE's tops are about 6 of their 9 us; the other 3 are open. *balanced* as a whole (3488.2) stayed in the band of its theory B. The combinations took 8 off the front and 14 to 26 off the tail: a median of 3466.1 (before, beside it, 3467.0) and 3466.8 (3467.5). That is some 0.8% better than the change and level with the kernel before, ratios 1.0000 and 0.9997. *combo3*'s tail (1389.2) and time (3466.1) lay nearer to theory L (1390 to 1398, 3464 to 3475) than to the full sum (1384, 3457). *combo4*'s tail lay below its expectation (1381.7 against 1384 to 1387), but its median did not fall with it (3460 to 3463 expected). No version here beats the kernel before.

## Why the prediction was wrong, point by point

The span was forecast to end at 3460.5 and ended at 3487.9, 27.4 later: 8.3 in G (inside its stated 2060 to 2085) and 19.1 in the tail (outside its 1378 to 1400). The other 7 of the median's error are, but for 1, the 6.0 that I took off because before's profiled span lay above its median; after's did not.

**Up to the head steps: right by the times forecast, by luck, and 5 us short by length.** First cache turn at 1811.3 (1812 said), merge at 1899.7 (1898), masks at 1938.8 (1940). But the latent queries came 6 us early, at 1798.0; in the control they came at 1810.1, and all of these 11 to 13 us later. Measured from them the merge came 101.7 us behind and not 94: TensorE waited 11.36 us for the first rows, and 4.84 for the second sample's (0 to 5 said, 1 taken). The first rows, issued at 1796.5 and 1797.7, took some 14 us to land (9 taken), with w_o and w_k issued 4 us behind them and the DMA share at 1.00; the second sample's were issued only at 1808.6, after the queries' store had landed. Keys and values were 3 us shorter. The rival of late cache rows had 10 us for this; some 9 came in the two waits, and 8 are left of them at the merge.

**Tile 5's front: the mis-sized term.** "3.84 us for four" query groups read a count of records as a count of matmuls; it is two groups. My own merge term had counted the same row rightly ("two times two query groups (7.7)"). 16 groups are 30 us of TensorE and not 15.4. In the row of after two head steps' query rows begin 5.42 us apart (2003.52 to 2008.94), and 3.74 of them are the two groups. By the masks, one a head step (L2962 before, L3231 after), head steps 23 to 37, in which the front of tile 5 stands, took 82.3 us and before 33.4: 48.9 more, where 35 had been said. Of these 6.5 are the norm and turn (5.5 said), 32.2 the eight steps with the queries and 10.2 the five behind them, in which the tops end and the projection takes 16.2 us for 13.9 at a lower granted clock. Nearly all of TensorE's time for the queries is thus paid, and the tops are not a cover for the later ones. The other head steps and the end took 3 less than before (1 more had been said), so that from the masks to G were 141.5 us in place of 132, 9.5 more. The masks of steps 23 and 37, before and then after:

```profile
1875.26 0.22 PE L2962 MATMUL psum<-arena 128*128 128x128 bf16 x1
1908.66 0.22 PE L2962 MATMUL psum<-arena 128*128 128x128 bf16 x1
```

```profile
1976.94 0.22 PE L3231 MATMUL psum<-arena 128*128 128x128 bf16 x1
2059.27 0.22 PE L3231 MATMUL psum<-arena 128*128 128x128 bf16 x1
```

**More bytes: right.** 4.5 MB and 11 us said; 4.27 MB and 10.4 us.

**The hole: about right.** Refill at G+27.3 (26.5 said), the bottom at 116 GB/s, 10.8 us alone in *late3* (9 said, bounds 5 and 12). That the second rival's slots behind it make it longer (56.8 in place of 50.0) was not seen, nor that before's own first 16 gathers had taken 52.9.

**Block 3 in 45 slots: the wrong step.** I had held that PE's average is under the pace and that six buffers even it out, and took 4 us. The rival "the mixed slots become the bound" had the place (slots 1 to 45, with waits between the engines), about the cycle (3.1 us; measured 3.09 and 3.10 over 32 slots, in two profiles) and the sign that VectorE waits for PE and not for gathers. It had them in part only: the share (0.8 to 0.9 said) was 0.78 and 0.94 over gathers 0 to 16 and 16 to 32, but 1.00 over 32 to 48, where VectorE waited 16.1 us for gathers beside the weights. That the mean comes to its 3.1 is partly luck, as the halves are 2.92 and 3.27. It was given 0.19. The busy times of my sum were near: for four slots TensorE had 9.2 us (9.0 said), VectorE 9.1 (10.0) and GpSimd 7.1 (6.8). What failed is the step from them to the pace: a sum of busy time under 10 us did not keep four slots at 10, for each pair of heads brings waits of one engine for another, and six buffers did not make them good. The rival's price, 27, came out at (3.09 - 2.45) x 32 = 21 over gathers 16 to 48 plus 7 in the first 16, but the 4 MB of weights lay hidden in the same slots, so the forecast's sum rises by less. *relief* and *tiny* show what taking much of the loop away gives back: 10 us at gather 128. Added to the forecast's terms that makes 345 + 10.4 for the bytes + 10.8 for the hole + 10 for the loop = 376, against 375.0 measured. The agreement is luck in part: before lost rate too, 410 against *ins4*'s 418 GB/s or 6 to 7 us. Taken from *ins4* the sum is 342.4 + 5.8 for 2.44 MB more + 10.8 + 10 = 369, and 6 us have no term of their own. By the rates of the rows, an estimate at 418 GB/s, the changed kernel lost 16 us in its first 16 slots, 7 in the next 16 and 4 in all the others.

**ACT's tables: costed at 0 to 2, worth about 4** (*notable*, one profile, with the earlier refill that may be up to 1.6 of it), since each load lies in the loop: behind the one the exponential waits, behind the other the Gelu of the next slot. The row repeats 1.28 us and the next activation 1.29 behind its start (2137.11 to 2138.40), so the Trainium skill's 2.66 us ("ScalarE: Activation LUTs", section "What ACT_TABLE_LOAD costs") is not what a switch takes here; its rule to batch activations by set ("Table sets: the hidden batching unit") did bear on this change, by up to 4 of the 33 us.

**Less work later: nothing said, 9 lost.** I had followed the 12 parts that leave the slots, not the 24 that land in tile 6's first 29 slots at 1.2 slots each. VectorE is at 89% there. *ins4* has the same 51.4, and *balanced*, with half of them there, 45.4: about 6 of the 9 are shown to be the tops.

Together: 1364.5 + 10.4 + 10.8 + 10 + 9 = 1404.7 for the tail, between the two profiles' 1403.4 and 1407.6, with the same luck in it. That block 3 in the slots makes the loss, that the dip is one part of it and the loop another, is shown by the kernels that take each away. The sizes are not exact to better than some 6 us, and how the loop's part divides between the four engines is not shown.

## What to carry to other kernels

When work is moved under a DMA-bound stream, and two engines are near the pace and their steps wait for each other in program order, what is hidden is not a sum of idle time: here 46 us of attention went under some 45 slots, in which TensorE and VectorE then showed 75% and 73% busy, and 33 to 37 came back as longer slots, a dip and bytes at full rate. And look at what the rest of the change costs alone: it was 36 us here, more than the move could pay. Price such slots by the nearest row in which the same kind of steps stand among slots (here 3.0 us, [rows 10]) and not by adding busy times. Count what a move leaves behind as well: tops that it pushes into the next tile, weights whose buffer is now free only when the stream is at full rate, and, before multiplying, check with a known count whether a row's x counts instructions or records.

## What the runs showed of the hardware that was not expected

A 128x128 f32 matmul with 128 columns leaves two records in the trace (64 for 32 instructions), each about 0.12 us of TensorE at the full clock (3.74 us for 32 records, granted clock 1.00).

POOL's scaling of 128x512 took between 3.11 us (at 2120.45) and 4.46 us (at 2130.66) for a pair, with nothing changed in its operands; why is open, and times on that engine are rough in this profile.

Where the bytes lay at the start of the stream decided what they cost. Query weights issued 4 us ahead of the first gather and 20 us behind it kept the transfers at 414 GB/s over the first 16 gathers (*ins4*), which moved 297 GB/s without them (after). 4 MB stored 1.5 us ahead of the ring's first refill made the first 16 gathers 6.4 us longer (*wqhole*). And 4 MB taken out of slots held near 3.1 us by the engines gave back 2.5 to 4.2.
